# Where the low parts of the last layer's weights are made: from GpSimd to VectorE, between the parts of the head normalisation

## The chip, the cores and the metric

The kernel runs on one core of one Trainium2 chip. The metric is the time of one execution on the device in microseconds (us), the median of several runs. The engines' names in the profile are PE (TensorE matmul), PEld (TensorE weight load), DVE (VectorE), ACT (ScalarE), POOL (GpSimd) and SP (SyncE, which issues the weight loads).

## The reference, cut to what matters

256 tokens of 1024 features pass through two layers of a first model (feed-forward, mixer, feed-forward), then through an "even" layer (a scan and dilated attention) and a last, "odd" layer. The change touches the odd layer alone:

```python
def moba_layer(x, norm_w, w_in, q_norm, k_norm, w_out, pos):
    h = rms_norm_2(x, norm_w)
    proj = jnp.einsum("bsd,df->bsf", h, w_in.astype(h.dtype))
    q, k, v, g = split_cols(proj, (MOBA_WIDTH,) * 4)          # 1024 columns each
    q = partial_rope_2(rms_norm_2(q.reshape(Bsz, S, 16, 64), q_norm), pos)
    k = partial_rope_2(rms_norm_2(k.reshape(Bsz, S, 16, 64), k_norm), pos)
    o = moba_attention(q, k, v).reshape(Bsz, S, MOBA_WIDTH) * jax.nn.silu(g)
    return x + jnp.einsum("bsf,fd->bsd", o, w_out)
```

With 256 tokens there is one block, so the attention is a plain causal softmax attention over 16 heads of 64.

## The kernel before

**Split weights.** A product with a weight matrix in float32 is made of three products in the faster fp32r type. A unit is 128 x 1024 weights in a slot of `ring`. ScalarE copies it rounded into `region_r` (the high part, `high_part`, L394; in the trace `region_r<-ring`); then VectorE or GpSimd subtracts the high part from the weights and writes the low part over them (`low_part`, L400; `ring_r<-ring,region_r`). TensorE takes a unit when the counter `l_ready` says that its low part is there. The units have one fixed order over the whole kernel: each low part waits for the high part of its unit, and the counters are plain counts, so units must be finished in their order. There are six places for high parts (`HIGHS`): the high part of unit u waits until TensorE is done with unit u-6 (`h_room`).

**The odd layer.** Every engine works through its own program in order, and semaphores join them; no scheduler moves anything. The order around the change is:

- VectorE and ScalarE normalise x, TensorE turns it (`norm`), and hH and hL (in the trace `hH` and `xs_r`) are the two parts of it.
- `token_blocks("ob", ...)` on TensorE: six blocks c = 0..5 of 512 columns (q: 0 and 1, k: 2 and 3, v: 4 and 5). Each block has 48 matmuls of 128 x 512 on four units, twelve to a unit; blocks 0 to 5 use units 0 to 23. ScalarE copies each block's two results out of psum (L1381) after the high parts that its program has before them.
- `heads_normed(2, 16, ...)` on VectorE, for q and then for k: the squares and their sums for both token tiles (L2039, L2042), the variance (L2047), then a wait for ScalarE's square root (`qk_roots`, L1565, which ScalarE has behind the copies of block 2 for q and of block 4 for k), a chain of short steps (L2049 to L2058), and for each token tile the scaling, the gains and the rotation (L2062, L2064, four short L2069, L2071, L2072).
- `heads_turned("moba", ...)` on TensorE: the transposes (L739) of the normalised q stand between blocks 4 and 5, those of k behind block 5. ScalarE copies them out (`region<-psum`), two at a time, since they have two psum banks.
- `attention("moba", ...)`: eight steps of two heads. In step s TensorE makes the scores of s (`Sb` on VectorE's side, L1760), one tile "og" of the output gate with unit 24+s (`out_gates`, 24 matmuls), the transposes of the probabilities of s-1 and the products with v of s-2. VectorE has `front(s)` (mask and maximum, L1760, and the negated maximum, L1771) and then `back(s-1)` (L1780, L1790, division by the sum). ScalarE has the exponentials of s (L1393), the high part of unit 28+s (s < 4), the copy of og, in steps 2, 5 and 7 a SiLU with its table loads, and the copies of the transposed probabilities.

GpSimd makes all low parts of the even layer and of the odd layer: 65 up to unit 1 of the odd layer, two parts of the normalised input (`norm_low(8)`, L406), and then the 30 that are left.

Of the kernel before, what the change touches and what calls it, by code (L numbers as in the profile page):

```python
# [55 lines left out]
SSD_H, DIL_H, MOBA_H = 16, 24, 16  # L56
# [40 lines left out]
AHEAD = 2  # L97
# [218 lines left out]
def build(nc, weights, par, par2, const, posts, x_in, mem_in, pos_in, out):  # L316
# [3 lines left out]
    with ctx:  # L320
# [367 lines left out]
        @block.gpsimd  # L688
        def _(pool):
            lay[0] = 0  # L690
            def norm_low(k):

                for half in range(2):
                    input_low(pool, k, 0, half)

            def lows(units):
                for u in units:
                    low_part(pool, u)

            lows(range(U_FFN1, U_FFN1 + AHEAD))  # L700

            def body():
                for j, slot in enumerate((0, 1, 0)):
                    norm_low(1 + j + 3 * lay[0])

                    pool.wait_ge(x_ready, 2 + 6 * lay[0] + (2 if j == 2 else 0))
                    pool.dma_start(gpost[:, slot, :], posts[3 * lay[0] + j].partition_broadcast(P))\
                        .then_inc(gp_full[slot], 16)
                    if j == 1:

                        pool.wait_ge(l_ready, Split(U_GATE).count - 1)
                        lows(GATE_UNITS + BRANCH_UNITS)
                        lows(range(U_FFN2, U_FFN2 + AHEAD))

                pool.wait_ge(l_ready, Split(3 * LAYER_CHUNKS).count - 1)
                lows(range(3 * LAYER_CHUNKS, 3 * LAYER_CHUNKS + AHEAD))

            layers(pool, body)
            norm_low(7)
            first_odd = N_EA + N_EB + AHEAD  # L720
            lows(TAIL_SPLIT[AHEAD:first_odd])
            norm_low(8)
            lows(TAIL_SPLIT[first_odd:])

        @block.tensor
# [914 lines left out]
        def _(dve):  # L1641
# [380 lines left out]
                    else:  # L2022
                        own(ins)

            def heads_normed(n, heads, copied, gains, pieces):

                width = heads * HD
                view = [[QK[:, qk, i, 0:width].rearrange("p (h d) -> p h d", h=heads) for i in range(NT)]
# [6 lines left out]
                for qk in range(2):  # L2035
                    for i in range(NT):
                        copied(qk, i)
                        own.settle()
                        own(dve.tensor_tensor(sq, QK[:, qk, i, 0:width], QK[:, qk, i, 0:width], ALU.mult))  # L2039
                        own.settle()  # L2040
                        at = (2 * qk + i) * heads
                        own(dve.tensor_reduce(sums[:, at:at + heads], sq.rearrange("p (h d) -> p h d", h=heads),  # L2042
                                              AX.X, ALU.add))
                    own.settle()
                    some = slice(2 * qk * heads, (2 * qk + 2) * heads)
                    total, v, root, r = (stat[:, j, some] for j in range(4))
                    dve.tensor_scalar(v, total, 1.0 / HD, EPS, ALU.mult, ALU.add).then_inc(qk_var, 1)  # L2047
                    dve.wait_ge(qk_std, 2 * n + qk - 1)
                    own(dve.reciprocal(r, root))  # L2049

                    own.settle()
                    own(dve.tensor_tensor(total, r, r, ALU.mult))
                    own.settle()
                    own(dve.tensor_tensor(total, total, v, ALU.mult))
                    own.settle()
                    own(dve.tensor_scalar(total, total, -0.5, 1.5, ALU.mult, ALU.add))
                    own.settle()
                    own(dve.tensor_tensor(r, r, total, ALU.mult))  # L2058
                    own.settle()
                    for i in range(NT):  # L2060
                        w = view[qk][i]
                        own(dve.tensor_tensor(w, w, bc(r[:, i * heads:(i + 1) * heads], 2, HD), ALU.mult))  # L2062
                        own.settle()
                        own(dve.tensor_tensor(w, w, bc(gains[qk], 1, heads), ALU.mult))  # L2064
                        own.settle()
                        a, b = w[:, :, 0:ROT], w[:, :, ROT:2 * ROT]
                        c, s = bc(cos2[:, i], 1, heads), bc(sin2[:, i], 1, heads)
                        for j, (u, z) in enumerate(((a, c), (b, s), (b, c), (a, s))):
                            own(dve.tensor_tensor(t_[:, j], u, z, ALU.mult))  # L2069
                        own.settle()  # L2070
                        own(dve.tensor_tensor(a, t_[:, 0], t_[:, 1], ALU.subtract))  # L2071
                        dve.tensor_tensor(b, t_[:, 2], t_[:, 3], ALU.add).then_inc(qk_ready, 1)  # L2072
                        dve.wait_ge(qk_ready, 4 * (n - 1) + 2 * qk + i + 1)

            def even_copied(qk, i):
                for c in range(3):
                    Job("eb", 3 * qk + c, i).wait_emptied(dve)

            heads_normed(1, DIL_H, even_copied, (A2("qn_dil"), A2("kn_dil")), 3)

            dt3 = dts[:, :, :].rearrange("p k (i h) -> p k i h", i=NT)
# [131 lines left out]
                for c in range(2):  # L2214
                    Job("ob", 2 * qk + c, i).wait_emptied(dve)

            heads_normed(2, MOBA_H, odd_copied, (A2("qn_moba"), A2("kn_moba")), 2)

            def odd_out(unit, job, rows):
                _, p, _ = unit  # L2220
                dve.wait_ge(og_ready, 1 + sum(p >= b for _, b in OG_SILU.values()))
                dve.tensor_tensor(mixedT[:, p, :], job.bank[:, 0:SEQ], ogT[:, p, :], ALU.mult).then_inc(job.free, 1)

            attention("moba", ODD_UNITS, odd_out)
            residual("odd_out")

# [197 lines left out]
```

## Time and profile before

| | |
|---|---|
| time, median of 3 runs | 2048.53 us (2047.55 to 2050.34) |
| time of the profiled execution | 2049.0 us |
| its span | 2047.3 us |
| busy TensorE | 1926.9 us, 94% |
| busy VectorE | 1068.4 us, 52% |
| busy ScalarE | 899.9 us, 44% |
| busy GpSimd | 456.1 us, 22% |
| the odd layer | from about 1870 us of the span to its end |

The profile lists instructions of one execution with their start from the span's start. A row of the time order reads: start, duration, engine, line, operation, what is written and read, how many merged instructions (xN; the duration is then that of all), and in brackets how long the engine stood idle before and whose work ended that. Most of the span is not touched by the change, so the shares of the whole span say little; the rows of the odd layer matter.

### The profile page before, as it was taken

What the parts mean: (1) busy time and instruction counts of PE and PEld (TensorE: products, weight loads), DVE (VectorE), ACT (ScalarE), POOL (GpSimd) and SP (SyncE); (2) the same over time, 40 slices, a digit from 0 to 9 for tenths busy, and PEclk for the clock granted to TensorE, in tenths of its full rate; (3) what the DMA queues carried; (4) which work ended last, traced back from release to release, by engine and by line L of the source; (5) the groups of instructions that cost most, each with busy time, mean ns of one, the idle gap of its engine ahead of it and who ended that gap; (6) DMA issues with size and microseconds to landing.
All of it is one profiled execution on the core that took longest, in us unless ns stands there. A gap on an engine that the chain in (4) does not pass through costs nothing. (4 is left out here: it accounts for less than half of the span.)

```text
span 2047.3 us, 31499 instructions
## 1 busy us (share of the span) xinstructions
PE 1926.9 (94%) x12048; PEld 1678.0 (82%) x12048; DVE 1068.4 (52%) x1887; ACT 899.9 (44%) x1386; POOL 456.1 (22%) x203
## 2 busy tenths in 40 slices
PE   6999999999899979999999999899888988999889
PEld 6999799988599969998999886899877867755665
DVE  7555561336355555554642344655484496651762
ACT  5443442784344444444335862444444433233363
POOL 1000001445100010000004443000066972004730
PEclk9999997999899979999997999899989998599999
DMA  6554446233354434544554324455434542004421
GB/s 275 185 184 184 174 177 241 99 124 124 134 185 184 184 135 179 185 185 170 186 214 156 118 97 150 168 184 186 157 124 149 190 154 93 1 1 151 157 93 52
DMA packets 29913, 311.69 MB, mean 152 GB/s; under 512 B 3312, under 2 KB 3696, under 8 KB 4848
## 3 DMA queue, kind: packets, MB, share of 16 engines
q1 hardware_dynamic: 28944, 307.13, 40.5%
q0 software_dynamic: 864, 3.15, 0.5%
q8 instruction: 68, 1.11, 0.2%
q14 instruction: 37, 0.30, 0.0%
HBM read 309.21 MB, written 1.05 MB: 152 GB/s over the span
## 5 line engine op out<-in xcount | busy, mean ns | idle before, releaser
L732 PE MATMUL psum<-hH,ring_r 128*128 128x256 f32 x2432 | 699.9, 288 | 0.0
L732 PE MATMUL psum<-hH,region_r 128*128 128x256 f32 x2336 | 668.4, 286 | 27.9 <-DVE xs_r L406 12.7
L732 PE MATMUL psum<-xs_r,region_r 128*128 128x256 f32 x2336 | 669.2, 286 | 0.0
L394 ACT ACTIVATE region_r<-ring 128x1024 fp32r<-128x1024 f32 x455 | 475.0, 1057 | 395.9 <-PE psum L732 341.9
L400 POOL TENSOR_TENSOR ring_r<-ring,region_r 128x1024 fp32r<-128x1024 f32 x141 | 344.5, 2466 | 1023.7 <-ACT region_r L394 1023.7
L400 DVE TENSOR_TENSOR ring_r<-ring,region_r 128x1024 fp32r<-128x1024 f32 x314 | 382.1, 1224 | 268.1 <-ACT region_r L394 252.1
L732 PEld LDWEIGHTS psum<-hH,region_r 128*128 128x128 f32 x2336 | 458.0, 196 | 42.6 <-issue 25.5
L732 PEld LDWEIGHTS psum<-hH,ring_r 128*128 128x128 f32 x2432 | 463.5, 191 | 0.0
L732 PEld LDWEIGHTS psum<-xs_r,region_r 128*128 128x128 f32 x2336 | 447.2, 191 | 4.4 <-issue 0.5
L732 PE MATMUL psum<-region_r 128*128 128x512 f32 x704 | 232.1, 392 | 0.0
L732 PE MATMUL psum<-region_r,hH 128*128 128x512 f32 (+3 forms) x512 | 160.4, 351 | 9.4 <-POOL ring_r L400 6.6
L732 PE MATMUL psum<-region_r,xs_r 128*128 128x512 f32 (+3 forms) x512 | 159.3, 349 | 0.2
L732 PEld LDWEIGHTS psum<-region_r 128*128 128x128 f32 x704 | 132.8, 189 | 26.3
L732 PE MATMUL psum<-ring,region 128*128 128x512 f32 x352 | 152.8, 593 | 0.8 <-DVE region L2191 0.8
L732 PE MATMUL psum<-ring_r,region_r 128*128 128x512 f32 x352 | 138.6, 394 | 0.0
L732 PEld LDWEIGHTS psum<-ring,region 128*128 128x128 f32 x352 | 66.5, 190 | 81.9 <-issue 80.3
L406 POOL TENSOR_TENSOR xs_r<-xs,hH 128x512 fp32r<-128x512 f32 x16 | 21.7, 1368 | 468.4 <-ACT hH L1346 468.3
L1381 ACT ACTIVATE region<-psum 128x256 f32<-128x256 f32 (+4 forms) x154 | 68.9, 453 | 125.2 <-PE psum L732 114.8
L732 PE MATMUL psum<-ring_r,hH 128*128 128x512 f32 (+2 forms) x320 | 123.6, 386 | 0.0
L1358 ACT ACTIVATE act<-psum 128x256 f32<-128x256 f32 x88 | 33.8, 384 | 193.7 <-PE psum L732 193.7
L732 PEld LDWEIGHTS psum<-region_r,hH 128*128 128x128 f32 x512 | 92.3, 194 | 24.3 <-POOL ring_r L400 7.1
L732 PEld LDWEIGHTS psum<-region_r,xs_r 128*128 128x128 f32 x512 | 92.3, 193 | 13.1 <-DVE region L1940 0.6
(200 smaller groups left out, 2138.9 us busy)
## 6 DMA issues: line engine op xcount, KB each, us to landing
ring<-in_weights SPq DMA_DIRECT2D x192, 1536.0 KB, 6.4
gpost<-in_posts POOLq DMA_DIRECT2D x6, 512.0 KB, 4.6
cst<-in_const SPq DMA_DIRECT2D x1, 1198.0 KB, 23.1
xs<-in_mem SPq DMA_DIRECT2D x1, 1024.0 KB, 5.6
x<-in_x SPq DMA_DIRECT2D x1, 1024.0 KB, 7.6
out<-x SPq DMA_DIRECT2D x2, 512.0 KB, 2.6
pars<-in_par SPq DMA_DIRECT2D x1, 336.0 KB, 8.0
p<-in_par SPq DMA_DIRECT2D x1, 204.0 KB, 24.8
```

What stands on the lines that cost most here:

```text
L394: eng.activation(unit.high, unit.raw, ACT.Copy).then_inc(h_ready, 1)
L400: eng.tensor_tensor(unit.low, unit.raw, unit.high.bitcast(F32), ALU.subtract).then_inc(l_ready, 1)
L406: eng.tensor_tensor(hL[:, i, ks, :], h_whole[:, i, ks, :], hH[:, i, ks, :].bitcast(F32), ALU.subtract)\
L732: ins = pe.matmul(bank, lhsT, rhs, start=start, stop=stop)
L1358: act_.activation(sil[:, t % 2, :], job.bank[:, 0:SEQ], ACT.Silu).then_inc(sil_ready, 1)
L1381: act_.activation(dst, src, func, **kw).then_inc(job.free, 1)
```

## The change

The last 30 low parts (units 2 to 31 of the odd layer) leave GpSimd's program, and VectorE gets them: ten ahead of the head normalisation, twelve between its parts, four behind it, and one in each of the steps 0 to 3 of the attention, behind `back(s-1)`. `heads_normed` gets a function `between` that is called behind each tile's squares and behind each normalised tile; in the even layer it is not given, and `pieces`, which was not used, is dropped. Units 0 and 1 of the odd layer and everything before stay on GpSimd.

```diff
@@ gpsimd @@
             lows(TAIL_SPLIT[AHEAD:first_odd])
             norm_low(8)
-            lows(TAIL_SPLIT[first_odd:])
@@ vector, heads_normed @@
-            def heads_normed(n, heads, copied, gains, pieces):
+            def heads_normed(n, heads, copied, gains, between=None):
...
                         own(dve.tensor_reduce(sums[:, at:at + heads], sq.rearrange("p (h d) -> p h d", h=heads),
                                               AX.X, ALU.add))
+                        if between is not None:
+                            between("squares", qk, i)
...
                         dve.wait_ge(qk_ready, 4 * (n - 1) + 2 * qk + i + 1)
+                        if between is not None:
+                            between("normed", qk, i)
@@ vector, odd layer @@
-            heads_normed(2, MOBA_H, odd_copied, (A2("qn_moba"), A2("kn_moba")), 2)
+            def odd_lows(lo, hi):
+                for u in TAIL_SPLIT[N_EA + N_EB + lo:N_EA + N_EB + hi]:
+                    low_part(dve, u)
+
+            ODD_LOWS = {("squares", 0, 1): (12, 16), ("normed", 0, 0): (16, 18), ("normed", 0, 1): (18, 20),
+                        ("squares", 1, 0): (20, 22), ("normed", 1, 0): (22, 24)}
+
+            def odd_between(*step):
+                if step in ODD_LOWS:
+                    odd_lows(*ODD_LOWS[step])
+
+            dve.wait_ge(l_ready, Split(U_OB + AHEAD).count - 1)
+            odd_lows(AHEAD, 12)
+            heads_normed(2, MOBA_H, odd_copied, (A2("qn_moba"), A2("kn_moba")), odd_between)
+            odd_lows(24, 28)
...
-            attention("moba", ODD_UNITS, odd_out)
+            def gate_lows(s):
+                if s + 4 < N_OA:
+                    odd_lows(28 + s, 29 + s)
+
+            attention("moba", ODD_UNITS, odd_out, gate_lows)
```

GpSimd's program ends, before the change, with the 65 low parts, the two input parts (L406) and the last 30:

```order
L406 TENSOR_TENSOR xs_r<-xs,hH 128x512 x2
L400 TENSOR_TENSOR ring_r<-ring,region_r 128x1024 x65
L406 TENSOR_TENSOR xs_r<-xs,hH 128x512 x2
L400 TENSOR_TENSOR ring_r<-ring,region_r 128x1024 x30
L320 UNCONDITIONAL_BRANCH
```

After the change the row of 30 is gone, and GpSimd has nothing in the odd layer behind the two input parts.

VectorE's program before the change, from the last part of the odd layer's input (L406) through q's squares, chain and first tile:

```order
L406 TENSOR_TENSOR xs_r<-xs,hH 128x512 x2
L2039 TENSOR_TENSOR Sb<-region 128x1024
L2042 TENSOR_REDUCE region<-Sb 128x16
L2039 TENSOR_TENSOR Sb<-region 128x1024
L2042 TENSOR_REDUCE region<-Sb 128x16
L2047 TENSOR_SCALAR region<-region 128x32
L2049 RECIPROCAL region<-region 128x32
```

The same place after the change (the lines are numbered one off, L2038 for L2039 and L2048 for L2047):

```order
L406 TENSOR_TENSOR xs_r<-xs,hH 128x512 x2
L400 TENSOR_TENSOR ring_r<-ring,region_r 128x1024 x10
L2038 TENSOR_TENSOR Sb<-region 128x1024
L2041 TENSOR_REDUCE region<-Sb 128x16
L2038 TENSOR_TENSOR Sb<-region 128x1024
L2041 TENSOR_REDUCE region<-Sb 128x16
L400 TENSOR_TENSOR ring_r<-ring,region_r 128x1024 x4
L2048 TENSOR_SCALAR region<-region 128x32
```

Ten low parts (units 2 to 11) now stand ahead of the squares and four (12 to 15) between them and the variance; in the same way two stand behind each of q's tiles, two behind k's first squares, and two behind k's first tile.

VectorE's program after the change between `front(1)` of the attention (its last instruction is the first row here) and `front(2)` (from the MEMSET on):

```order
L1770 TENSOR_SCALAR small<-small 128x4
L1779 RECIPROCAL small<-small 128x4
L1789 TENSOR_SCALAR Sb<-Sb,small 128x128
L1789 TENSOR_SCALAR Sb<-Sb,small 128x256
L1789 TENSOR_SCALAR Sb<-Sb,small 128x128
L1789 TENSOR_SCALAR Sb<-Sb,small 128x256
L400 TENSOR_TENSOR ring_r<-ring,region_r 128x1024
L1751 MEMSET small 128x1
```

The low part of unit 29 is new there; it comes behind `back(0)` and ahead of `front(2)`, and waits for ScalarE's high part of that unit.

## Rows read from the trace of the kernel before

**Rows 1.** The page: its first line.
```profile
span 2047.3 us, 31499 instructions
```

**Rows 2.** Waits in the odd layer: total us, times, longest.
```profile
ACT region L1565 <- DVE region L2047: 9.6, 1, 9.6
...
PE psum L739 <- DVE region L2072: 8.7, 2, 5.0
...
PE psum L739 <- ACT region L1381: 4.1, 1, 4.1
```

**Rows 3.** TensorE in time order, 1940 to 1969 us: start, duration, work.
```profile
1940.49 1.94 PE L739 MATMUL psum<-cst,region 128*128 128x128 f32 x8 [5.05 <-DVE region L2072]
1946.48 1.97 PE L739 MATMUL psum<-cst,region 128*128 128x128 f32 x8 [4.05 <-ACT region L1381]
1948.10 0.78 PE L732 MATMUL psum<-region_r,hH 128*128 128x512 f32 x1
...
1964.03 3.50 PE L739 MATMUL psum<-cst,region 128*128 128x128 f32 x16 [3.63 <-DVE region L2072]
1968.26 0.93 PE L732 MATMUL psum<-region 64*128 64x128 f32 x8 [0.73 <-ACT region L1381]
```

**Rows 4.** VectorE in time order, head normalisation.
```profile
1902.03 1.22 DVE L2039 TENSOR_TENSOR Sb<-region 128x1024 f32<-128x1024 f32 x1 [24.71 <-issue]
...
1904.64 2.52 DVE L2039 TENSOR_TENSOR Sb<-region 128x1024 f32<-128x1024 f32 x1
1907.20 1.22 DVE L2042 TENSOR_REDUCE region<-Sb 128x16 f32<-128x1024 f32 x1
...
1924.15 9.62 DVE L2069 TENSOR_TENSOR Sb<-region,cst 128x128 f32<-128x128 f32 x4
...
1936.40 1.22 DVE L2062 TENSOR_TENSOR region<-region 128x1024 f32<-128x1024 f32 x1
...
1938.91 0.90 DVE L2069 TENSOR_TENSOR Sb<-region,cst 128x128 f32<-128x128 f32 x4
...
1940.38 1.22 DVE L2039 TENSOR_TENSOR Sb<-region 128x1024 f32<-128x1024 f32 x1
...
1947.26 1.22 DVE L2062 TENSOR_TENSOR region<-region 128x1024 f32<-128x1024 f32 x1
```

**Rows 5.** GpSimd in time order.
```profile
1903.67 10.46 POOL L400 TENSOR_TENSOR ring_r<-ring,region_r 128x1024 fp32r<-128x1024 f32 x4 [1.68 <-ACT region_r L394]
1914.93 21.08 POOL L400 TENSOR_TENSOR ring_r<-ring,region_r 128x1024 fp32r<-128x1024 f32 x8 [0.80 <-ACT region_r L394]
1950.11 9.64 POOL L400 TENSOR_TENSOR ring_r<-ring,region_r 128x1024 fp32r<-128x1024 f32 x4 [14.10 <-ACT region_r L394]
...
1991.73 2.39 POOL L400 TENSOR_TENSOR ring_r<-ring,region_r 128x1024 fp32r<-128x1024 f32 x1 [5.00 <-ACT region_r L394]
```

**Rows 6.** The page, part 5: low parts on VectorE, whole span.
```profile
L400 DVE TENSOR_TENSOR ring_r<-ring,region_r 128x1024 fp32r<-128x1024 f32 x314 | 382.1, 1224 | 268.1 <-ACT region_r L394 252.1
```

**Rows 7.** ScalarE in time order, blocks 2, 4 and 5.
```profile
1912.48 1.30 ACT L1381 ACTIVATE region<-psum 128x512 f32<-128x512 f32 x2 [3.52 <-PE psum L732]
...
1934.78 1.30 ACT L1381 ACTIVATE region<-psum 128x512 f32<-128x512 f32 x2 [3.52 <-PE psum L732]
1945.71 0.23 ACT L1565 ACTIVATE region<-region 128x32 f32<-128x32 f32 x1 [9.64 <-DVE region L2047]
...
1959.73 1.29 ACT L1381 ACTIVATE region<-psum 128x512 f32<-128x512 f32 x2 [3.52 <-PE psum L732]
```

**Rows 8.** VectorE by line, the attention from 1968 to 2014 us.
```profile
L1771 DVE TENSOR_SCALAR small<-small 128x4 f32<-128x4 f32 x8 | 5.9, 740 | 0.3
```

**Rows 9.** ScalarE in time order: the high part in step 0 of the attention.
```profile
1972.55 1.04 ACT L394 ACTIVATE region_r<-ring 128x1024 fp32r<-128x1024 f32 x1
```

**Rows 10.** VectorE in time order: front(1) begins.
```profile
1973.15 0.29 DVE L1760 CUSTOM_DVE_ANT_0 Sb<-psum,cst 128x128 f32<-128x128 f32 x1 [2.41 <-issue]
```

**Rows 11.** TensorE in time order: the transposes of step 3's probabilities.
```profile
1995.32 0.88 PE L739 MATMUL psum<-cst,Sb 128*128 128x128 f32 x6 [1.75 <-DVE Sb L1790]
```

More of the change, by code:

```diff
@@ L2077, in even_copied @@
                     Job("eb", 3 * qk + c, i).wait_emptied(dve)
-            heads_normed(1, DIL_H, even_copied, (A2("qn_dil"), A2("kn_dil")), 3)
+            heads_normed(1, DIL_H, even_copied, (A2("qn_dil"), A2("kn_dil")))
             dt3 = dts[:, :, :].rearrange("p k (i h) -> p k i h", i=NT)
```

## The prediction

> **What bounds the kernel now.** I read the waits of the odd layer first, then TensorE's rows in time order, then those of VectorE and GpSimd beside each other. TensorE sets the time, so what counts is where it stands still. Three waits stand out [rows 2]: 8.7 us for VectorE's last rotation (two times, the longer 5.0), 4.1 us for a copy of ScalarE, and, one step behind, ScalarE's own 9.6 us for VectorE's variance. In time order [rows 3]: at 1940.49 TensorE had stood 5.05 us before it could turn q; at 1946.48 it had stood another 4.05 us, because ScalarE could not empty the two banks of the transposes: its program has k's square root ahead of that copy, and the root began at 1945.71, after a wait of 9.64 us for the variance [rows 7]. At 1964.03 it had stood 3.63 us until k was normalised, and only at 1968.26 did the scores begin. All three waits are for one thing: VectorE's head normalisation is late.
>
> Why is it late? The reader should lay VectorE's rows beside GpSimd's. Four short rotations take 9.62 us at 1924.15 and 0.90 us at 1938.91 [rows 4]. GpSimd runs eight low parts from 1914.93 to 1936.01 [rows 5], 2.6 us each; the slow rows lie inside this stretch, the fast ones behind it. 9.62 / 4 = 2.4 us is one low part on GpSimd: each of these VectorE instructions waits for about a whole GpSimd instruction, whatever its own size. The sum over 1024 columns at 1907.20 takes its usual 1.22 us while GpSimd runs (from 1903.67 to 1914.13), whereas the square ahead of it takes 2.52. So it is the operations with two inputs in the on-chip memory that are held up, and the reduction is not. The rows say the time: all of q and k takes VectorE from 1902.03 to 1964.0, 62 us.
>
> The Trainium skill, in "SBUF — State Buffer", section "Who interferes with whom", says that a VectorE instruction with two SBUF inputs and a GpSimd instruction that reads SBUF exclude each other for a whole instruction, and that a `tensor_reduce` never takes part. The trace agrees in both. The same page's summary advises to put "whichever is off the critical path" behind the other, which speaks against more work on the late engine; by it the lows would stay on GpSimd, and the sum would be no gain. The third rival below, which is worked out from rows, is that case.
>
> **The change, part by part.** Prices first, all from stretches in which GpSimd is silent. A low part on VectorE is 1.224 us, the mean of 314 [rows 6]; with the gap between instructions I take 1.25. One normalised tile (L2062 to L2072) is 1936.40 to 1940.38, 3.98 us. Squares of two tiles and the variance, up to the start of ScalarE's root, are 1940.38 to 1945.71, 5.33 us; root and chain 1945.71 to 1947.26, 1.55 us [rows 4, 7].
>
> *Removed.* All 30 low parts of GpSimd in the odd layer, and with them each hold-up of VectorE from 1877 us on. GpSimd then has nothing to do, no DMA or wait of its own goes with them, and no load on SP waits for it: a slot is given back by TensorE.
>
> *Units 2 to 11, ahead of the squares.* VectorE has stood 24.71 us before 1902.03 [rows 4] waiting for block 1 of TensorE and its copies, and these ten cost 12.5 us spread over that time. Behind them VectorE waits only for high parts that ScalarE makes before the same copies. So the squares start at 1902.03 as now: cost nothing. Were the cover gone, it would be up to 12.5 us.
>
> *From the squares on,* adding durations: squares of q to 1907.2 (now slowed by one GpSimd instruction), units 12 to 15 to 1912.2, variance 1912.4. ScalarE is free for the root at 1912.48 + 1.30 = 1913.8 [rows 7], so this root stays where it is; cost of the four low parts nothing, with 1.4 us of slack. Then, from the chain's end: 1915.2, tile 0 to 1919.2, units 16 and 17 to 1921.7, tile 1 to 1925.7. **q is ready at 1925.7 instead of 1940.4.** TensorE ends block 4 at about 1934.8 (ScalarE's copy starts at 1934.78) and turns q at once; the 5.05 us wait goes, with 9 us to spare.
>
> Units 18, 19 to 1928.2; first squares of k 1930.8; units 20, 21 to 1933.3; second squares and variance 1935.9. ScalarE is free for k's root at 1934.78 + 1.30 = 1936.1. That is nearly a tie (0.2 us), and it is the place to watch: every microsecond that VectorE is later delays TensorE by one. With the root at 1936.1 block 5 starts as long behind it as now, 1948.10 - 1945.71 = 2.4 us, so at **1938.5 instead of 1948.10**.
>
> Chain to 1937.6, tile 0 of k 1941.6, units 22, 23 to 1944.1, tile 1 to **1948.1**. Block 5 takes 1934.78 - 1912.48 = 22.30 us for two blocks, so 11.15 us, or 11.63 us as block 5 did itself (1948.10 to ScalarE's copy at 1959.73); I take 11.4. So the copy comes at 1949.9 and TensorE is free at about 1950.3: k has been ready for 2 us, and the 3.63 us wait goes too. Turning k up to the scores is bound by ScalarE's copies, 1968.26 - 1964.03 = 4.23 us, so the scores begin at **1954.5 instead of 1968.26: 13.8 us earlier**.
>
> Does TensorE have to wait for a low part? Its need is 2.8 us per unit (11.15 / 4). Unit 12 is ready at 1908.5, needed at 1912.5; unit 16 at 1920.5, needed at 1923.6; unit 18 at 1927.0, needed at 1929.2; unit 22 at 1942.9, needed at 1938.5 + 5.7 = 1944.2. The least slack is 1.3 us; cost nothing, else what goes beyond it. Units 24 to 27 are done at 1948.1 + 5 = 1953.1, ahead of front(0) at about 1955.5.
>
> *Units 28 to 31, in the attention.* Here a wait is added: VectorE waits for ScalarE's high part, which comes behind the exponentials of the same step, and front(s+1), queued behind it, waits as well, and TensorE for that. In step 0 the high part ends at 1972.55 + 1.04 = 1973.6 [rows 9], then the low part 1.2: front(1) would start at 1974.85 instead of 1973.15 [rows 10], 1.7 us later. Against it stands what goes: the negated maxima (L1771) take 740 ns in the mean [rows 8] for about 170 ns of work, so GpSimd holds up the eight by 4.6 us in all, always between front and back. Bounds: if the low parts are hidden and all hold-ups were on the path, -4.6 us; if none were and each of the four low parts costs 1.7, +6.8 us. Going through the steps: in step 1 the later front (+1.7) almost meets the hold-up (-1.5), in step 2 it is +0.5 altogether, in step 3 ScalarE's table loads set the pace, and in step 4 front(4) is 2.6 us later, of which 2.0 are a hold-up that goes. The transposes at 1995.32 [rows 11] come 0.7 us later against the scores, and the rest keeps its pace. I take **+0.7**.
>
> *Sum.* -13.8 + 0.7 = -13.1 us. Against the profiled execution, span 2047.3 [rows 1] and time 2049.0 (1.7 more), the span would be 2034.2 and the time 2035.9. The median of the runs is 0.5 below that execution: **2035.5 us**.
>
> **The rivals.**
>
> *VectorE late by 2 to 5 us* (chance 0.17). The low parts, with their semaphore waits, take more than 1.25 us, or the root of k is not met. With 10 low parts between 1907 and k's variance, 0.3 us more each is 3 us, of which all but 0.2 reaches TensorE: 2038.5. For it: the tie. Against it: nothing else shares VectorE's memory path then.
>
> *More than the sum* (chance 0.10). The attention comes out at its lower side, -1 to -3 us instead of +0.7, and block 5 takes 11.15: 2032 to 2034. Against it: the high part ends after TensorE has offered scores(1).
>
> *VectorE becomes the bound: slower* (chance 0.03). If the slow rows are not GpSimd's doing, VectorE keeps its 62 us and gets 12 low parts more, 15 us: k ready at 1979 instead of 1964, and the attention pays +6.8, so 2048.5 + 15 + 7 = 2070. The point from which it decides: k may be 15.9 us later than I say (1948.1 against 1964.0) before the gain is gone, which is 2.6 us per low part in place of 1.25, the pace of GpSimd. Against it: the four rotations at 1938.91, 0.90 us with GpSimd silent, on the same tiles with TensorE and ScalarE at work.
>
> *The gain is lost later, no change* (chance 0.02). TensorE reaches the gate or output weights before their loads. These loads are asked for when TensorE frees a slot, so they move along with it; 2048.5.
>
> **How the numbers follow.** The likeliest case (chance 0.68) is the sum, 2035.5; its own range, from ties and block 5, is 2034 to 2037.5. The range for 8 in 10 takes in part of both neighbours: 2032.5 to 2039.5. About 0.2% (4 us) is what a measurement here can tell from no change. Faster by more: 0.68 + 0.17 + 0.10 and a little off for mishaps, 0.95; within 0.2%: 0.02; slower: 0.03.
>
> **What would show it.** In the changed kernel's profile: four L2070 in 0.9 us each time; variance of k at about 1935.9 and ScalarE's wait for it near zero; no 5.05 and 4.05 us before the transposes; block 5 from 1938.5; scores from 1954.5; L1770 at 0.17 us; low parts on VectorE at 1.22 us. Wrong would be: TensorE waiting for low parts within a block; the variance of k behind 1938; front(s+1) more than 2 us behind TensorE's scores in steps 1 to 4.

## The result, and the profile after

The changed kernel takes 2033.13 us (median of 4 runs, 2028.82 to 2035.37), the kernel before took 2048.5 us beside it (2047.55 to 2050.34). The ratio is 0.9921, with a 95% interval of 0.9904 to 0.9939: faster by 12.5 to 19.7 us. The forecast was 13.1 us less and 2035.5 us. The forecast gain lies inside the measured interval, but the middle of that interval, 0.79% or 16.2 us, is three microseconds beyond it. Taken by the ratio, the new time is 0.9921 x 2048.5 = 2032.3 us, just below the forecast range of 2032.5 to 2039.5 us. Direction and mechanism came out, one size did not.

The waits of the odd layer after the change, in total us, times and longest:

```profile
PE psum L738 <- DVE Sb L1789: 3.9, 3, 2.1
...
DVE region L2050 <- ACT region L1564: 3.3, 2, 2.2
...
PE psum L731 <- ACT region L1380: 0.7, 1, 0.7
PE psum L738 <- ACT region L1380: 0.7, 2, 0.4
```

The 8.7 us of TensorE for the rotation and the 9.6 us of ScalarE for the variance [rows 2] are gone from the list, and the 4.1 us for a copy is 0.7 us in two pieces. VectorE still waits for ScalarE's two roots, 3.3 us in all. Left on TensorE is a wait inside the attention, 3.9 us for the divided probabilities, which was 3.4 us before.

TensorE in time order, where it turns q and k and begins the attention:

```profile
1935.62 1.04 PE L738 MATMUL psum<-cst,region 128*128 128x128 f32 x8
1937.08 1.14 PE L738 MATMUL psum<-cst,region 128*128 128x128 f32 x8 [0.42 <-ACT region L1380]
...
1949.20 1.03 PE L738 MATMUL psum<-cst,region 128*128 128x128 f32 x8
1950.54 1.15 PE L738 MATMUL psum<-cst,region 128*128 128x128 f32 x8 [0.30 <-ACT region L1380]
1952.42 0.93 PE L731 MATMUL psum<-region 64*128 64x128 f32 x8 [0.73 <-ACT region L1380]
```

These are the rows that stood at 1940.49, 1946.48, 1964.03 and 1968.26 [rows 3]. No transpose waits for VectorE any more. The reader should also see the durations: eight transposes took 1.94 us before and take 1.04 now. The instructions are the same. The windows say why (us, busy PE and instructions, granted clock, DMA share, GB/s), first of the kernel before:

```profile
1940.00:1948.10 8.10, 3.56 (x16) 0.50 0.00 0
1948.10:1959.70 11.60, 11.60 (x48) 0.92 0.38 136
1964.00:1968.20 4.20, 3.50 (x16) 0.63 0.60 185
```

and the same three pieces of work after the change:

```profile
1935.30:1938.20 2.90, 2.48 (x20) 1.00 0.28 119
1938.20:1948.70 10.50, 10.50 (x47) 1.00 0.41 150
1948.70:1952.40 3.70, 2.69 (x19) 1.00 0.46 137
```

Before, TensorE's granted clock was 0.50, the level of 1.2 GHz, when it came out of its waits of 5.05 and 4.05 us, and block 5 ran at 0.92 in the mean; now all three stretches run at 1.00, the level of 2.4 GHz.

VectorE in time order, from behind q's squares to k's variance:

```profile
1907.39 4.63 DVE L400 TENSOR_TENSOR ring_r<-ring,region_r 128x1024 fp32r<-128x1024 f32 x4
...
1925.48 0.29 DVE L2073 TENSOR_TENSOR region<-Sb 128x128 f32<-128x128 f32 x1
1925.80 2.36 DVE L400 TENSOR_TENSOR ring_r<-ring,region_r 128x1024 fp32r<-128x1024 f32 x2
...
1935.25 0.18 DVE L2048 TENSOR_SCALAR region<-region 128x32 f32<-128x32 f32 x1
1936.57 0.35 DVE L2050 RECIPROCAL region<-region 128x32 f32<-128x32 f32 x1 [1.14 <-ACT region L1564]
...
1940.37 0.90 DVE L2070 TENSOR_TENSOR Sb<-region,cst 128x128 f32<-128x128 f32 x4
```

and ScalarE's copies of blocks 4 and 5 and its root for k. The head part is measured from the copy of block 4 to the first scores:

```profile
1935.13 1.29 ACT L1380 ACTIVATE region<-psum 128x512 f32<-128x512 f32 x2 [3.51 <-PE psum L731]
1936.31 0.22 ACT L1564 ACTIVATE region<-region 128x32 f32<-128x32 f32 x1
...
1948.71 2.27 ACT L1380 ACTIVATE region<-psum 128x512 f32<-128x512 f32 x4 [3.52 <-PE psum L731]
```

A group of four low parts takes 4.63 us, so each 1.16 us instead of the 1.25 that the forecast took. Adding the rows of the two profiled executions gives where the 13.8 us between their spans (2047.3 and 2033.5) come from:

| stretch | before | after | difference |
|---|---|---|---|
| up to ScalarE's copy of block 4 | 1934.78 | 1935.13 | +0.35 |
| from there to the first scores | 33.48 | 17.29 | -16.19 |
| to the transposes of step 3 | 27.06 | 27.55 | +0.49 |
| to the end | 51.98 | 53.53 | +1.55 |

### The profile page after: what moved, and what is told of

It is laid out like the page before. It is cut to its first block, busy times and chain, and to the rows that moved or that the text cites. A ratio compares the mean times of both kernels' runs of the same rounds, so it can differ in the third digit from the quotient of the medians.

```text
span 2033.5 us, 31502 instructions
## 1 busy us (share of the span) xinstructions
PE 1924.1 (95%) x12048; PEld 1675.7 (82%) x12048; DVE 1070.4 (53%) x1917; ACT 899.5 (44%) x1386; POOL 381.7 (19%) x173
## 4 chain that ended last, share of the span: by engine, by line
PE 58%; DVE 8%; issue 6%; ACT 3%; POOL 1%; DVEq 0%; ACTq 0%; POOLq 0%
PE psum L731 56%; PE psum L738 2%; DVE Sb L2018 1%; POOL ring_r L400 1%; DVE Sb L2015 1%; ACT region_r L394 1%; DVE Sb L2070 1%; DVE ring_r L400 1%; DVE Sb L1759 1%; DVE region L2065 1%; DVE region L2063 0%; ACT Sb L1392 0%; DVE xs L1694 0%; DVE x L1701 0%; DVE xs L1664 0%
## 5 line engine op out<-in xcount | busy, mean ns | idle before, releaser
L400 DVE TENSOR_TENSOR ring_r<-ring,region_r 128x1024 fp32r<-128x1024 f32 x344 | 417.5, 1223 | 288.1 <-ACT region_r L394 271.7
L400 POOL TENSOR_TENSOR ring_r<-ring,region_r 128x1024 fp32r<-128x1024 f32 x111 | 270.2, 2458 | 979.9 <-ACT region_r L394 979.9
L406 POOL TENSOR_TENSOR xs_r<-xs,hH 128x512 fp32r<-128x512 f32 x16 | 21.7, 1370 | 469.1 <-ACT hH L1345 469.0
```

Source lines behind the costliest of these rows:

```text
L400: eng.tensor_tensor(unit.low, unit.raw, unit.high.bitcast(F32), ALU.subtract).then_inc(l_ready, 1)
L406: eng.tensor_tensor(hL[:, i, ks, :], h_whole[:, i, ks, :], hH[:, i, ks, :].bitcast(F32), ALU.subtract)\
```

## The experiments

**The changed kernel once more**, without an edit.

> The changed kernel once more, with more rounds, to know its time and how it spreads. Both theories: a profiled span of 2031 to 2034 us, a ratio of 0.992 to 0.993 to the kernel before. Theory A (the wait's end also keeps TensorE's clock up, and a late front in step 4 of the attention lets it fall): the transposes of q and k take 1.0 us per 8 and not 1.9; in executions of about 2031 us the half clock near 1980 us of the span is absent or shorter. Theory B (what goes beyond the forecast is a difference of the executions ahead of the odd layer): the scores begin 16.2 us ahead of before only in some executions.

Measured: 2033.21 us (2029.31 to 2034.4), ratio 0.9929, interval 0.9916 to 0.9942. The profiled span was 2027.4 us, below the 2031 to 2034 us expected and 6.1 us less than that of the first. The stretches say where: its copy of block 4 came 4.55 us earlier (1930.58), copy to first scores is 17.30 us (17.29), scores to the transposes of step 3 27.56 us (27.55), and the rest 51.96 us (53.53). So the two stretches in which the change moved work repeat within 0.01 us, and the spread of the times lies ahead of the odd layer and in one place behind. That place is the +1.55 us in the last row of the table: behind the same 2.10 us wait the clock fell in one execution and not in the other. The first trace:

```profile
1979.97 0.88 PE L738 MATMUL psum<-cst,Sb 128*128 128x128 f32 x6 [2.10 <-DVE Sb L1789]
...
1981.96 1.66 PE L731 MATMUL psum<-region 64*128 64x128 f32 x8
```

These scores take 0.93 us elsewhere, and the window behind the wait has a granted clock of 0.65:

```profile
1979.90:1984.00 4.10, 4.03 (x24) 0.65 0.01 4
```

In the second trace:

```profile
1975.44 0.88 PE L738 MATMUL psum<-cst,Sb 128*128 128x128 f32 x6 [2.10 <-DVE Sb L1789]
...
1980.89 0.82 PE L738 MATMUL psum<-cst,Sb 128*128 128x128 f32 x6
```

Here the window at the same place of the program has 1.00, and the next transposes come 5.45 us later, against 6.99 us in the first:

```profile
1975.30:1979.40 4.10, 3.96 (x34) 1.00 0.01 4
```

The +1.55 us is not quite free of the change, as the traces of all kernels here show together. The change lengthened this wait from 1.75 to 2.10 us. Six traces have a wait of 2.10 to 2.12 us there. In four of them (the changed kernel, the two kernels with extra instructions, and the one with writes on GpSimd) the clock fell, to 0.58 to 0.65, and the rest took 53.5 to 53.6 us. In the other two it took 52.0 us. In the seven traces with a wait of 1.78 us or less, the kernel before among them, the rest took 51.9 to 52.3 us each time. So the longer wait has a price of 1.5 us in some executions. How often is known only from these six.

**GpSimd busy again, with work that nobody needs.** Thirty operations of GpSimd with two inputs in the on-chip memory, on a buffer that is free in this stage; VectorE, ScalarE and TensorE keep the changed program.

```diff
+            for n, u in enumerate(TAIL_SPLIT[first_odd:]):
+                pool.wait_ge(h_ready, Split(u).count)
+                pool.wait_ge(idle_work, n)
+                pool.tensor_tensor(gpost[:, 1, :], gpost[:, 0, :], gpost[:, 0, :], ALU.subtract).then_inc(idle_work, 1)
```

> The changed kernel, and GpSimd, which is idle there, gets 30 instructions of the old shape and pace (128 x 1024, two inputs in the on-chip memory, each behind the high part of its unit), on a buffer that nobody uses. Nobody waits for them. Theory (VectorE's two-input instructions are held up by GpSimd's instructions, whatever these compute): the short L2070 rows take 2.4 us each again, VectorE's twelve low parts are held up too, k is ready 25 to 40 us later, and the kernel is slower than before: 2055 to 2075 us. Rival (the waits came from who made the low parts, or from the ring's memory): 2033 as the changed kernel.

Measured: 2056.68 us (2053.82 to 2057.17), ratio 1.0042, interval 1.0027 to 1.0056: slower than the kernel before. VectorE's rows are held up again, although it uses nothing of GpSimd's:

```profile
1923.65 4.17 DVE L2075 TENSOR_TENSOR Sb<-region,cst 128x128 f32<-128x128 f32 x4
...
1933.48 2.80 DVE L2070 TENSOR_TENSOR region<-region,p 128x1024 f32<-128x1024 f32 x1
1936.31 0.90 DVE L2075 TENSOR_TENSOR Sb<-region,cst 128x128 f32<-128x128 f32 x4
1937.24 1.94 DVE L2077 TENSOR_TENSOR region<-Sb 128x128 f32<-128x128 f32 x1
```

Four rotations take 4.17 us beside GpSimd and 0.90 us in a pause of it, and the product with the gains (L2070 here), 1.22 us by itself, takes 2.80. The hold-up is smaller than expected: 4.17 us for four rotations and not 9.6, and k is ready at 1967.7, 20 us later than in the changed kernel and not 25 to 40. The time lies in the expected range all the same, because VectorE is now late with the low parts too: TensorE stood still for them four times, 15.9 us in all, the longest 8.62 us at 1931.23.

**The same with writes only.** The operation above is replaced by a memset of twice the columns.

```diff
+                pool.memset(gpost[:, :, :], 0.0).then_inc(idle_work, 1)
```

> The same, but GpSimd's 30 instructions only write (a memset of 128 x 2048): no input. If the hold-up is of reads, as the rule of the Trainium skill has it (SBUF page, Who interferes with whom), nothing is held up: 2031 to 2035, L2070 at 0.9 us for four. If any GpSimd instruction holds VectorE up: above 2045.

Measured: 2033.73 us (2031.96 to 2033.94), ratio 0.9927, interval 0.9911 to 0.9944: the time of the changed kernel. GpSimd is busy, four memsets in 7.61 us:

```profile
1913.77 7.61 POOL L727 MEMSET gpost<- 128x2048 f32 x4 [3.65 <-ACT region_r L394]
```

and VectorE beside it is not held up:

```profile
1916.81 0.69 DVE L2075 TENSOR_TENSOR Sb<-region,cst 128x128 f32<-128x128 f32 x3
```

Three of the four rotations, all that this view has, in 0.69 us are the usual 0.23 each. Together the two runs show that neither GpSimd being at work nor a wait for its results is enough to hold VectorE up, and that GpSimd's instructions with inputs from the on-chip memory are. The Trainium skill, "SBUF — State Buffer", section "Who interferes with whom", names the same pair of instructions; both runs agree with it.

**k's variance later, twice.** The tie between k's variance and the end of ScalarE's copy was "the place to watch". Two extra instructions of 1.2 us stand behind k's first squares, and in a second kernel six. The diff is that of the six; only these are each waited for:

```diff
+                if step == ("squares", 1, 0):
+                    for n in range(6):
+                        own(dve.tensor_tensor(gpost[:, n % 2, :], x[:, 0, :], x[:, 1, :], ALU.subtract))
+                        own.settle()
```

> Two more VectorE instructions of 1.22 us with two inputs, 2.3 to 2.5 us together, behind the first squares of k, where the changed kernel has 1.1 us between k's variance and ScalarE's root. Theory A (VectorE and ScalarE nearly tie there): root and block 5 1.2 to 1.4 us later, and TensorE's wait before the second pair of transposes grows from 0.4 to 1.8 us; 1.2 to 2 us slower than the changed kernel, more if the clock falls. Rival (VectorE has room): 0.

> Six more VectorE instructions of 1.23 us, each awaited (7.5 us), behind k's first squares, where two more cost TensorE 1.4 us of waiting and no clock. TensorE then stands about 7 us ahead of the second pair of transposes. Theory (a stand of 4 us and more lets the clock fall to 1.2 GHz, and that was the part of the gain which the forecast left out): the transposes take 1.9 instead of 1.1 us per 8, block 5 starts 2.3 to 2.4 us behind the root instead of 1.66, lasts 11.6 us instead of 10.7; scores 8 to 9 us later than in the changed kernel, not 6.4. Rival (only the wait counts): 6.4 us.

Measured with two: 2033.85 us (2031.95 to 2035.72), ratio 0.9934, interval 0.9921 to 0.9948. The time can't be told from the changed kernel's, but the trace can: copy to scores 18.71 us instead of 17.29, so 1.42 us later for 2.27 us of work between the squares. The rest, 0.85 us, is the slack that the changed kernel had: its variance began at 1935.25, and ScalarE was only free at 1936.31 (with the two, variance and root are 0.22 us apart). With six: 2042.84 us (2039.49 to 2044.19), ratio 0.9972, interval 0.996 to 0.9983. ScalarE waits for the variance and TensorE for ScalarE:

```profile
1943.29 0.23 ACT L1564 ACTIVATE region<-region 128x32 f32<-128x32 f32 x1 [6.69 <-DVE region L2048]
```

```profile
1944.06 1.97 PE L738 MATMUL psum<-cst,region 128*128 128x128 f32 x8 [7.22 <-ACT region L1380]
```

Copy to scores is 25.91 us, 8.62 us more than in the changed kernel. The root accounts for 6.81 of them (it began 7.99 us behind the copy instead of 1.18). The other 1.81 us lie between root and the copy of block 5, 14.21 us instead of 12.40, with the same work in it: these transposes take 1.97 us instead of 1.14, and the window from 1938 to 1951 has a granted clock of 0.74. This is a piece that the forecast missed: here a wait of 7.22 us cost TensorE its length and then nearly 2 us at the lower clock. The 4 us in the expectation are no measured threshold: in the kernel before, the clock was at 0.63 behind a wait of 3.63 us, and behind 2.10 us it fell in some executions.

**The price of the last layer's low parts on VectorE.** In this kernel the low parts of units 2 to 31 are not made at all; TensorE reads the high part in their place, so the output lacks the low parts' share. VectorE has only a one-column memset for each.

```diff
-                    low_part(dve, u)
+                    dve.wait_ge(h_ready, Split(u).count)
+                    dve.wait_ge(l_ready, Split(u).count - 1)
+                    dve.memset(small[:, 53:54], 0.0).then_inc(l_ready, 1)
```

> Nobody makes the low parts of units 2 to 31: VectorE only counts them up with a write of one column at the same places, and TensorE reads the high part a second time instead (the same matmuls; the output lacks the low parts' share). Theory (the twelve low parts between 1902 and 1948 us are hidden under TensorE's blocks, those of the attention are not): scores within 0.3 us of the changed kernel's, the attention 0.5 to 3 us shorter, 2030 to 2033. Rival (the lows on VectorE still cost time in the head part): scores 2 us or more earlier.

Measured: 2027.68 us (2027.28 to 2031.12), ratio 0.9905, interval 0.9887 to 0.9923. Copy to scores is 17.29 us, to the hundredth that of the changed kernel: the 26 low parts ahead of the attention cost nothing. From the scores to the end it is 76.54 us against 79.52 in the repeated run. The three microseconds are the price of making the four low parts of the attention, not of the waits for their high parts, since this kernel keeps those waits:

```profile
1963.38 0.06 DVE L2226 MEMSET small<- 128x1 f32 x1 [1.79 <-ACT region_r L396]
```

Scores to the transposes of step 3 is 24.29 us here, 3.27 us less than with the low parts made (27.56).

**Units 28 to 31 back on GpSimd.**

```diff
@@ gpsimd @@
+            pool.wait_ge(l_ready, Split(U_OA + 4).count - 1)
+            lows(range(U_OA + 4, U_OA + N_OA))
@@ vector, gate_lows @@
-                if s + 4 < N_OA:
-                    odd_lows(28 + s, 29 + s)
+                pass
```

> Only the low parts of units 2 to 27 on VectorE; those of 28 to 31 are GpSimd's again. Theory A: scores at 1952.4 as in the changed kernel, then the attention of before: L1770 at about 700 ns, the transposes of step 3 at +27.1 us; if the clock falls only when the wait reaches 2.1 us, it stays up here and the span is 2031.5 to 2032; otherwise 2033. Rival (GpSimd's instructions hold up the attention by more than the added waits cost): 2035.

Measured: 2029.62 us (2029.31 to 2033.14), ratio 0.992, interval 0.9906 to 0.9934: no difference from the changed kernel. Scores to the transposes of step 3 is 26.98 us (27.56). GpSimd's four take 2.38 us each and hold VectorE up in the steps as before: the four negated maxima beside them take 1.68, 1.15, 0.20 and 2.20 us instead of 0.17. The last of them, beside the low part on GpSimd:

```profile
1972.38 2.38 POOL L400 TENSOR_TENSOR ring_r<-ring,region_r 128x1024 fp32r<-128x1024 f32 x1 [5.00 <-ACT region_r L394]
1972.59 2.20 DVE L1772 TENSOR_SCALAR small<-small 128x4 f32<-128x4 f32 x1
```

**The same four one step later on VectorE.** The wait in the attention is for the high part of the same step. Here VectorE makes each low part a step later, when its high part has long been there.

```diff
-                if s + 4 < N_OA:
-                    odd_lows(28 + s, 29 + s)
+                if 1 <= s and s + 3 < N_OA:
+                    odd_lows(27 + s, 28 + s)
```

> The low part of unit 28+s is made one step later, when its high part is long there, so front(s+1) no longer waits for ScalarE. Theory A: no wait of VectorE for ScalarE's high part in the attention; the transposes of step 3's probabilities come 25 to 27 us behind the first scores (27.55 in the changed kernel), TensorE's wait there falls below 1.5 us and its clock stays at 2.4 GHz; 1.5 to 3 us faster than the changed kernel, span 2030 to 2032. Rival: ScalarE's table loads in step 2 set the pace of step 3 and 4, and nothing is gained: 2033.

> The run with the gate's low parts one step later once more, without any edit, beside the even layer's edit on the same chip. It should give 2027.9 +- 1.5, ratio 0.991, and if the theory of the attention holds again no wait of TensorE in steps 1 to 3 and 23.0 us from the first scores to the transposes of step 3. If that 23.0 was chance of one execution, it is 27 here.

Measured: 2027.86 us (2025.26 to 2028.98), ratio 0.9907, interval 0.9892 to 0.9922; and in a second run of it, beside the even layer's edit below, 2025.89 us (2023.4 to 2029.17), ratio 0.9884, interval 0.9869 to 0.9899. VectorE in the changed kernel:

```profile
1957.65 1.23 DVE L400 TENSOR_TENSOR ring_r<-ring,region_r 128x1024 fp32r<-128x1024 f32 x1 [2.88 <-ACT region_r L394]
...
1975.91 1.23 DVE L400 TENSOR_TENSOR ring_r<-ring,region_r 128x1024 fp32r<-128x1024 f32 x1 [3.70 <-ACT region_r L394]
```

and with the edit, from the second trace:

```profile
1959.67 1.22 DVE L400 TENSOR_TENSOR ring_r<-ring,region_r 128x1024 fp32r<-128x1024 f32 x1
1964.24 1.22 DVE L400 TENSOR_TENSOR ring_r<-ring,region_r 128x1024 fp32r<-128x1024 f32 x1
1969.77 1.22 DVE L400 TENSOR_TENSOR ring_r<-ring,region_r 128x1024 fp32r<-128x1024 f32 x1
1975.13 1.22 DVE L400 TENSOR_TENSOR ring_r<-ring,region_r 128x1024 fp32r<-128x1024 f32 x1
```

No low part waits, and TensorE has no wait for the probabilities. Scores to the transposes of step 3 is 22.99 us in one trace and 23.02 in the other, 4.5 us less than in the changed kernel (27.55, 27.56). That is more than expected (25 to 27 us, and 1.5 to 3 us of time; the medians differ by 5.3 us). Of the 4.5 us, 3.3 are the low parts themselves, which stood between the wait and the next scores, and 1.3 the bare waits (24.29 us in the kernel that makes no low parts). The kernel before paid 4.1 us (27.06) for GpSimd's hold-ups.

**Units 2 to 11 back on GpSimd**, ahead of the head normalisation.

```diff
@@ gpsimd @@
+            lows(TAIL_SPLIT[first_odd:N_EA + N_EB + 12])
@@ vector @@
-            dve.wait_ge(l_ready, Split(U_OB + AHEAD).count - 1)
-            odd_lows(AHEAD, 12)
+            dve.wait_ge(l_ready, Split(U_OB + 12).count - 1)
```

> The changed kernel with units 2 to 11 of the odd layer back on GpSimd, which is then done at about 1902, before VectorE's first squares of q, or a few us behind them. Prediction's step (those ten cost nothing on VectorE and gain nothing there): copy of block 4 to first scores 17.3 us as in the changed kernel, time the same within 0.2%, 2033 +- 3. Rival (GpSimd is not done when the squares of q start, since it begins only when its high parts are there, and holds up one or two of them): VectorE is up to 3 us late at q's variance, of which up to 1.4 us are covered; 0 to 1.5 us slower.

Measured: 2033.04 us (2029.73 to 2033.61), ratio 0.9918, interval 0.9903 to 0.9933. Copy to scores is 17.31 us, the attention 27.56 us: these ten cost nothing on VectorE, and their move gained nothing. What is left for the 16.2 us from copy to scores is the sixteen low parts (units 12 to 27) that no longer run on GpSimd beside the normalisation.

**The even layer too.** It has the same construction, with 45 units, and its trace the same signs: TensorE stood 6.7 us at 1667 for GpSimd's low part, ScalarE 13.5 us for the variance. On top of the edit of one step later, VectorE makes these low parts between the parts of that layer's normalisation.

```diff
+            EVEN_LOWS = {("squares", 0, 1): (16, 20), ("normed", 0, 0): (20, 24), ("normed", 0, 1): (24, 28),
+                         ("squares", 1, 0): (28, 32), ("chain", 1, 0): (32, 36), ("normed", 1, 0): (36, 38)}
...
+            even_lows(0, 16)
+            heads_normed(1, DIL_H, even_copied, (A2("qn_dil"), A2("kn_dil")), even_between)
+            even_lows(38, N_EB)
```

> As the run with the gate's low parts one step later, and the even layer's 45 low parts made on VectorE too: sixteen ahead of its head normalisation, 22 between its parts (one group of four between the variance and the chain), seven behind; GpSimd keeps the 18 low parts of the block before it and the first two of the odd layer. Theory (VectorE's two-input instructions are held up by GpSimd's low parts in the even layer just as they were in the odd one): there TensorE stood 6.7 us at about 1667 for a low part of GpSimd, and ScalarE 13.5 us for VectorE's variance; four short rotations took 9.9 us. They take 0.9 us, the 6.7 us wait is gone and some 1 us of half clock behind it, so 7 to 8 us less than the run without this edit: about 2020, ratio 0.987. Rival (the even layer's wait was for GpSimd's low part itself and not for the normalisation, and VectorE is as late with 38 low parts in its way as GpSimd was): TensorE waits for low parts of VectorE within the blocks, 0 to 3 us gained: 2025 to 2028. Rival with the other sign: the normalisation of k is now later than before and the transposes wait; over 2030.

Measured: 2016.8 us (2014.88 to 2017.36), ratio 0.9842, interval 0.9829 to 0.9856; the kernel without this edit was 2025.89 us on the same chip, so 9.1 us less, a little more than the 7 to 8 us expected. That kernel's windows around the wait (columns as above):

```profile
1640.00:1665.00 25.00, 20.95 (x91) 0.99 0.53 189
1665.00:1680.00 15.00, 12.36 (x46) 0.79 0.27 105
```

and with the even layer's edit:

```profile
1640.00:1665.00 25.00, 25.00 (x109) 1.00 0.51 190
1665.00:1680.00 15.00, 15.00 (x67) 1.00 0.57 210
```

The idle time is gone and the clock stays up. The next copy of a block comes at 1671.57 instead of 1680.13, 8.56 us earlier: 6.7 us of wait and 1.9 us of clock. This is the fastest version that was tried, 1.6% below the kernel before.

## Where the prediction was right, and the step that failed

- **The cause of the late normalisation** was right: hold-ups by GpSimd's reads. Unneeded GpSimd instructions with inputs bring them back, and writing ones do not. Too narrow was "the operations with two inputs": the negated maximum, with one, was held up as well (740 ns in the mean [rows 8] instead of 170), which the forecast priced but did not explain. The rival in which VectorE becomes the bound needed the slow rows to be something else, and they were not.
- **The low parts' places** were right: q ready at 1925.8 (forecast 1925.7), k at 1948.1 (1948.1), k's variance done at 1935.4 (1935.9). That q and k came out so well hides two small errors. The low parts were 0.09 us shorter each than priced, and q's root waited for ScalarE's copy, which came 0.35 us later with all that stands ahead of it. The rival "VectorE late by 2 to 5 us" did not occur; the run with two extra instructions shows 0.85 us of slack where the forecast had 0.2.
- **The failed step** is the size of "the scores begin at 1954.5 instead of 1968.26: 13.8 us earlier". It measured 16.2 us. That is the term of the sum that was mis-sized. Three parts of it were too long: block 5, counted from the root to ScalarE's copy, 12.40 us instead of 13.8 (-1.4); turning k up to the scores, taken from before as 4.23 us and with the copy ahead of it 4.6, in fact 3.71 (-0.9); and the root 1.18 us behind the copy instead of 1.30 (-0.1). The first two have one main cause. Their durations were read from rows of before that ran behind a wait of TensorE, at a granted clock of 0.50, 0.92 and 0.63, and used for a kernel in which those waits are gone, and with them the lower clock. The rows for it stood in the forecast (eight transposes in 1.94 us, sixteen in 3.50), but the windows with their clock were not read beside them. The run with six extra instructions shows that the wait is the cause: it brings back the 1.97 us transposes and 1.8 us of the loss. Not all of it is the clock. Of the 1.4 us, 0.7 are the second transposes of q (block 5 begins 1.66 us behind the root, not 2.4) and 0.7 the block, 10.74 us from its first matmul to the copy against the 11.4 taken. The lower value weighed for it, 11.15, came from copy to copy at full clock. It was still 0.4 us too long, because the copy begins before the block's last matmuls do (1948.71 against 1948.97).
- **The attention, +0.7 us,** measured +0.5 us in both traces up to the transposes of step 3. The net was right up to there and also its two sides, the hold-ups that go (L1770 takes 0.17 us now) and the waits for the high parts that come. What was not seen is that either is worth about 4 us and that both can be avoided. "The rest keeps its pace" held in one trace of the two; in the other the lower clock behind the longer wait added 1.55 us.
- **A sign of being wrong** appeared without the forecast being wrong in that place: front(1) began 2.50 us and front(4) 3.52 us behind the start of TensorE's scores, where more than 2 us was to speak against it. The sign did not fit the forecast's own working, in which front(1) came 1.7 us and front(4) 2.6 us later than before; they came 1.5 and 2.4 us later.
- **The reading of the Trainium skill's summary** ("SBUF — State Buffer"), that the low parts should stay on GpSimd, was the prediction's own inference, and here it would have been the wrong choice. The third rival was not that case either: it supposes that the slow rows are not GpSimd's doing, and they were.
- **A slip in the chances:** 0.68 + 0.17 + 0.10 already give 0.95, so nothing was taken off for mishaps.
- **"More than the sum"** was forecast with the attention below zero and a shorter block 5. Block 5 was shorter, the attention was not below zero.
- The gain of 13.1 us and the measured one also differ by chance of the executions: the ratio gives 16.2 us, that of the repeated run 14.5 us (0.9929), the two profiled executions 13.8 and 19.9 us. The two traces agree to 0.01 us from copy to scores and up to the transposes of step 3. They differ by 4.55 us ahead of the odd layer and by 1.57 us behind the 2.10 us wait. Why an execution takes one course or the other in these places stays open.

## What to carry to other kernels

When a wait of TensorE goes, take the durations behind it from a stretch that ran at the full granted clock: the gain is the wait plus what the lower clock cost. Between block 4's copy and the scores TensorE stood 13.5 us before and 1.5 us after, so 12.0 of the 16.2 us are waits. Nearly all of the other 4.2 us are the same work done faster: 1.6 us in q's transposes, 0.9 in block 5 and 1.3 in k's transposes. In the even layer it was 1.9 us beside 6.7. Elementwise work with inputs from the on-chip memory on GpSimd can cost VectorE's instructions up to a whole GpSimd instruction each (four of 0.23 us took 9.62 us in one place and 5.31 in another), so it may be cheaper to give the work to the engine that looks late, as long as pieces of 1.2 us fit between its steps. Where an added wait is for a result of the same pipeline step, move the waiting instruction one step on: that was worth 4.5 us here and needed no other change. It also took away the wait of TensorE behind which the clock fell in some executions.

## What the hardware showed that was not expected

- The clock does not always fall behind the same wait. Behind 2.10 us before the transposes of step 3 the granted clock was 0.65 in one trace and 1.00 in another of the same program, at 1.54 us of time. The Trainium skill, "TensorE: Matmul & The Clock Gate", section "Part 1: The HAM clock gate (the "warmup" mystery)", says that an idle TensorE goes to the lower level and that how much work runs at it afterwards differs from run to run. The first trace shows such work behind the wait; in the second no work behind it ran at the lower level.
- The time also differs from execution to execution at a place that no edit touches and that has no wait of TensorE before it, two copies of the even layer's 16-column results: they lie 2.68 us apart in seven of the thirteen traces and 4.6 to 5.1 us in the other six, where the granted clock over the stretch of one of them (1703 to 1713 us) was 0.62. With its 2 us or so, that is one source of a spread of some 4.5 us between executions of one kernel (2029.3 and 2033 to 2034 us for the changed one).
- A memset on GpSimd of 128 x 2048, 1.9 us, leaves VectorE's two-input instructions as they are; a subtraction of 128 x 1024 does not.
